# Layer 1's second query slot (QB) among the projections ahead of the scan in place of beside it, in a two-layer hybrid backbone on one core

## What is computed

```python
px = (h_x * (1.0 + ca_x) + sa_x) @ w_in[l]          # all slots of a layer at once
pc = (h_c * (1.0 + ca_c) + sa_c) @ w_in[l]
(qa, ka, va, qb, kb, vb, qc, ic, fcf, fcb, gc, qd, kd, vd) = _split_cols(px)
# group B: queries and keys with a norm per head, then the rotation
o_b = _global_attn_latent(_rope2d(nq(qb), cos, sin), _rope2d(nk(kb), cos, sin), _heads(vb), kb_c, vb_c)
# group C: a gated scan in both directions, context first, then latent tokens
f = lbd + (1.0 - lbd) * jax.nn.sigmoid(zf.astype(f32))      # zf is fcf or fcb
s_new = jnp.exp(b_last)[..., None] * s + jnp.einsum('blhk,blhv->bhkv', kc * jnp.exp(b_last[:, None] - b), vc)
```

## Time and profile before

| what | us |
|---|---|
| median of 3 runs | 2049.73 |
| lowest and highest of them | 2046.92, 2051.88 |
| the profiled execution | 2052.52 |
| its span in the profile | 2050.9 |
| TensorE busy in the span | 1927.3 |
| VectorE, GpSimd, ScalarE busy | 1294.1, 907.0, 898.8 |

### The profile page before, as it was taken

One profiled execution on the slowest core, in us unless ns is written; L12 is line 12 of the kernel. 1 busy time (PEld: TensorE's weight loads), 2 busy tenths in 40 slices (PEclk: granted clock), 3 DMA queues, 4 the chain that ended last, 5 costly groups with the idle time before them and its releaser, 6 DMA issues.

```text
span 2050.9 us, 33287 instructions
## 1 busy us (share of the span) xinstructions
PE 1927.3 (94%) x12872; PEld 1642.2 (80%) x12872; DVE 1294.1 (63%) x2519; ACT 898.8 (44%) x1917; POOL 907.0 (44%) x700
## 2 busy tenths in 40 slices
PE   6898999999999999999999998898989989999997
PEld 4787888877788888888888878798867868778886
DVE  3237888775586999999444362988786752222545
ACT  3224577567634222222243343565557534333442
POOL 2134566210154334553353334666340445675743
PEclk8999899999999999999999999999999999999999
DMA  8553010030111233323211121111130112222321
GB/s 340 204 210 122 22 43 22 22 119 2 43 62 42 106 121 124 124 87 129 93 67 68 52 103 62 42 43 42 43 119 2 63 62 99 87 87 98 124 99 66
DMA packets 26940, 177.33 MB, mean 86 GB/s; under 512 B 2720, under 2 KB 3744, under 8 KB 7712
## 3 DMA queue, kind: packets, MB, share of 16 engines
q1 hardware_dynamic: 22544, 157.90, 21.3%
q10 hardware_dynamic: 4240, 17.30, 2.1%
HBM read 171.00 MB, written 4.19 MB: 85 GB/s over the span
## 4 chain that ended last, share of the span: by engine, by line
PE 68%; DVE 15%; issue 5%; POOL 5%; ACT 4%; DMA 2%; DVEq 0%; SPq 0%; ACTq 0%; POOLq 0%
PE PS L1257 19%; PE PS L1156 18%; PE PS L872 7%; PE PS L866 5%; PE PS L1092 3%; PE PS L1117 3%; POOL WS L2341 3%; DVE W L1678 2%; DMA WR<-in_weights 2%; PE PS L1076 2%; DVE W L1995 2%; DVE W L1942 2%; PE PS L801 1%; PE PS L1005 1%; PE PS L1212 1%
## 5 line engine op out<-in xcount | busy, mean ns | idle before, releaser
L1257 PE MATMUL PS<-XH,WS 128*128 128x512 f32 x2016 | 544.5, 357 | 4.7 <-POOL WS L2341 4.7
L1257 PEld LDWEIGHTS PS<-XH,WS 128*128 128x128 f32 x2016 | 360.7, 190 | 60.4 <-issue 4.6
L1257 PE MATMUL PS<-XL,WS 128*128 128x512 f32 x1008 | 358.7, 356 | 0.0
L2341 POOL TENSOR_TENSOR WS<-WR,WS 128x1024 fp32r<-128x1024 f32 x88 | 214.8, 2442 | 295.9 <-ACT WS L1536 295.5
L1601 ACT ACTIVATE W<-PS,PR 128x768 f32<-128x768 f32 (+1 forms) x88 | 78.0, 886 | 431.3 <-PE PS L1257 362.8
L2200 DVE SCALAR_TENSOR_TENSOR W<-PS,PR,W 128x511 f32<-128x511 f32 (+1 forms) x132 | 83.0, 657 | 219.2 <-ACT W L1601 219.2
L1257 PEld LDWEIGHTS PS<-XL,WS 128*128 128x128 f32 x1008 | 191.8, 190 | 26.8
L872 PE MATMUL PS<-EU,XH 128*128 128x256 f32 x624 | 186.6, 299 | 8.0 <-issue 7.3
L2301 POOL TENSOR_TENSOR WL<-WR,EU 128x512 fp32r<-128x512 f32 x96 | 127.7, 1356 | 141.3 <-ACT EU L1316 141.1
L872 PE MATMUL PS<-WL,XH 128*128 128x256 f32 x624 | 180.6, 289 | 0.0
L872 PE MATMUL PS<-EU,HL 128*128 128x256 f32 x624 | 180.4, 289 | 0.0
(11 more groups left out here) (219 smaller groups left out, 4256.9 us busy)
## 6 DMA issues: line engine op xcount, KB each, us to landing
WR<-in_weights SPq DMA_DIRECT2D x128, 1024.0 KB, 4.8
U<-in_weights SPq DMA_DIRECT2D x16, 1024.0 KB, 6.9
U<-in_bias ACTq DMA_DIRECT2D x2, 1792.0 KB, 9.7
H<-in_x SPq DMA_DIRECT2D x1, 2048.0 KB, 10.1
H<-in_x ACTq DMA_DIRECT2D x1, 2048.0 KB, 15.1
U<-in_ln_rows ACTq DMA_DIRECT2D x2, 1024.0 KB, 4.7
WR<-in_weights SPq DMA_DIRECT2D x4, 512.0 KB, 3.6
kept<-H ACTq DMA_DIRECT2D x4, 512.0 KB, 2.6
```

Source lines behind the costliest of these rows:

```text
L1257: mm = pe.matmul(PS[u.pos][:, lo:hi], w[:, part, k, :], src[:, k, lo:hi], start=(k == 0 and src is xh3 and part == 0), stop=(k == KT - 1 a ...
L2341: pool.tensor_tensor(ws5[:, u.c % 2, 1], half_slot(u), ws5[:, u.c % 2, 0], ALU.subtract).then_inc(w_low, 1)
```

## The change

One row of the table `ORDERS` changes: in layer 1, QB moves from behind KVA to ahead of FCF.

```diff
 ORDERS = ((QC, GC, IC, QB, KVB, FCF, FCB, QA, KVA, VD, QD, KD),
-          (QC, GC, IC, FCF, FCB, QA, KVA, QB, KVB, VD, QD, KD))
+          (QC, GC, IC, QB, FCF, FCB, QA, KVA, KVB, VD, QD, KD))
```

## The result

| what | before | after |
|---|---|---|
| median of 3 runs, us | 2049.73 | 2067.50 |
| lowest and highest, us | 2046.92, 2051.88 | 2065.31, 2070.59 |
| span of the profiled execution, us | 2050.9 | 2063.7 |
| ratio after to before (95% interval) | | 1.0075 (1.0057 to 1.0093) |

The change makes the kernel slower by 0.75%, 15.4 us by the ratio and 17.8 by the medians. The prediction said slower, by 6 us, and its range ended at 2064: the sign was right and the size was not.

The account below looks back on a forecast made before the run. TensorE, busy 94% of the span, was taken as the bound. Ahead of the scan 62.0 us plus scan 164.3 made 226.3 against 220.7, about 6 us more: 2055.7 us from the median 2049.7, range 2046.5 to 2064.

Parts of the forecast that it names:

- (1): Ahead of the scan, after QB's first part: TensorE waits 0.7 us for FCF's low halves on GpSimd; between 0 and 0.8.
- (2): Ahead of the scan, past FCF's second context part: TensorE waits 0.5 us for QB's first part's rotation; between 0 and 1.
- (3): Behind FCF's first latent part: TensorE waits 6.5 us for QB's second rotation, slowed beside GpSimd's FCB low halves; 2.4 to 7.
- (4): Before FCB's first latent part: TensorE waits 4.4 us for ScalarE's take of FCB's context parts; between 3.5 and 4.8.
- the clock: Behind waits (3) and (4), ahead of the scan: lower clock costs 2 us each; between 0 and 2.6 each.
- Together 164.3: The whole scan, layer 1, to the first attention score: 164.3 us; bounds 158.5 and 171.
- iterations 0 to 3 ... 18.6: Scan's start: 11 pieces of 1.45 us and four small steps on TensorE, 18.6 us.
- 4 to 11 ... 60.0: Scan iterations 4 to 11: 5.4, 8.0, six at 7.43, and 2 for transposes, 60.0 us, against 71.8 before.
- 12 to 15: ... no wait ... 19.5: Second direction's context units: 10 pieces and small steps, no wait, 19.5 us, against 33.0 before.
- 16 to the end ... 66.2: Scan from iteration 16 to its end: 5.8, six at 8.1, 11.8, sum 66.2 us, against 72.1 before.
- D: Rival, scan: loop at 8.27 us in all sixteen output units, iteration 16 waits for ScalarE; +12 to +15; chance 0.11.
- B: Rival: no meeting in QB's second rotation, clock at 2.4 GHz, units at 7.2 to 7.6; -8 us; chance 0.12.

Follow-up runs that it names:

- e3: Changed kernel with FCB's weights split two parts later, behind own part 11 in place of 9; ratio 1.0060.
- e4: Changed kernel with ScalarE taking FCB's two context parts ahead of unit 0's exponentials in layer 1; ratio 1.0082.
- e9: e2's kernel with ScalarE's takes of FCB's context parts ahead of unit 0's exponentials; ratio 1.0000.
- e7: Changed kernel with layer 1's KVA weights split at iterations 0 and 1 and QD's at 13, each one earlier; ratio 1.0061.
- e5: Changed kernel with layer 1's KVA weights split at iterations 0 and 1 in place of 1 and 2; ratio 1.0070.
- e14: Kernel before the change, with ScalarE's copy of turned keys ahead of the exponentials for units 12 to 15 (also 2 and 3); ratio 0.9997.
- e15: e8's kernel with ScalarE's copy of turned keys ahead of the exponentials for units 12 to 15 (also 2 and 3); ratio 1.0056.
- e6: Changed kernel with layer 1's QD weights split at iteration 13 in place of 14; ratio 1.0063.
- e11: e8's kernel with the reciprocals of FCB's latent gates on VectorE replaced by a minimum (result invalid); ratio 0.9994.
- e12: Changed kernel with 24 unread products put into TensorE's 6.57 us wait before the transposes of QB part 2; ratio 1.0084.
- e8: Changed kernel with the edits of e3, e4 and e7 together (four edits); ratio 1.0033.
- e10: e8's kernel with VectorE's norm and rotation of layer 1's KVA and KVB replaced by a copy (result invalid); ratio 1.0015.
- e13: e8's kernel with TensorE leaving out one of three products per step for layer 1's KVA and KVB; ratio 1.0028.
- e2: Kernel before the change, QB still beside the scan, with only the changed kernel's staging of layer 1's forget gates; ratio 1.0007.

## Why the prediction was off, point by point

**The stretch was the right one.** 16.8 us of the difference lie in it; in front of it and behind the scores the programs differ by less than their executions do (the profiled one of after reaches the first mark 2.6 us earlier, and takes 556.7 against 558.1 from the scores on).

**The moved work and the four waits ahead of the scan** came out as written: (1) 0.67 for 0.7, (2) none for 0.5, (3) 6.57 for 6.5, (4) 4.44 for 4.4, the clock 2.9 and 1.7 for 4, and 62.9 us from IC's end (1271.71 less the 2.57 that after is ahead, to 1332.04) for 62.0. Two sizes inside (3) are off and cancel, so that its agreement is in part luck: the rotation was slowed by 3.2 us, not 4.2, and FCF's gate before it by 1.0 (1.45 for a row that alone takes 0.41). That the mechanism of (3) is the meeting, e3 shows; that (4) is the place of the take, e4 shows, and that it is worth nothing on its own, e4 and e9.

**The scan is the step that failed:** "Together 164.3", measured 174.5 (1332.04 to 1506.5), 10.2 of the 11 us by which the sum of 226.3 was short. By its four terms:
- "iterations 0 to 3 ... 18.6": 23.9. The 3.48 us wait for KVA's low halves, 0.58 for a copy, and 1.7 for 3.4 us at the lower clock. I priced it as TensorE's work and did not walk the splits of weights, which the change also moves, through ScalarE's and GpSimd's queues.
- "4 to 11 ... 60.0": 59.4.
- "12 to 15: ... no wait ... 19.5": 23.0. A wait of 3.12 and its clock.
- "16 to the end ... 66.2": 68.2 to the end of the projections, 68.7 to the scores.

**But the error was deeper than two overlooked waits.** With both edited, e7's units 0 to 3 take 18.1, below my 18.6, and its second direction 65.9, and still the scan is 171.3, the upper bound that I had given: units 4 to 15 take 87.8 for my 79.5. The first and the last term were within reach and the sum was not: I had costed them as if a wait taken out of the scan were taken out of the total. Most edits of order contradict that: 6.3 us of gain ahead of the scan gave nothing (e4), 5.8 in units 0 to 3 nothing (e5), nor did 4.7 in e9 or the copies in e14 and e15. Two did keep their gain, e3's 3.6 ahead of the scan and e6's 2.9 in the second direction. What it is in the scan that takes the others back, the two engines' loads together, the chain through a unit, or the clock that falls behind the new waits, stays open; e5 shows the clock with 3.1 of 4.8 us. The kernel before idles 17.8 us in its scan and the kernel after 15.3, though 27 us of TensorE's busy time and 34 of VectorE's have left it.

**The clock:** I had 4 us ahead of the scan, which came out, and none in it. The mean went from 0.96 to 0.93 over the whole stretch, and the same products took 7.6 us more. In the scan there are more and shorter waits, and several are followed by the lower level.

**The rivals.** D came nearest in size (+12 to +15), but not by its mechanism: the units of 4 to 11 take 7.4 us (59.4 for eight) and those of 16 to 22 7.7, not 8.27, and the stall stands at iteration 15, for unit 14's copy, not at 16. B needed no meeting and units at 7.2 to 7.6; even with the meeting gone (e3) it is far off, since the shortest scan with the changed order took 171 us (e7, e11), not 158.5.

**What stays open.** e12 and after run the same instructions from unit 16 on and differ by 4.3 us; so a difference of that size in one stretch of one profile is no proof. The 4.8 us that e5 loses behind units 0 to 3 stand better, since e7 repeats them (87.8 for units 4 to 15). e6's 2.9 us are repeated too: the six kernels with QD split earlier and nothing else moved there (e6, e7, e8, e10, e11, e13) take 65.6 to 66.2 us from unit 16 on, the five with QD's split as it was (after, e3, e4, e5, e12) 68.7 to 73.0. Not run is a kernel that lightens TensorE and VectorE at once. Why e2, with QB in the scan, gives TensorE no more idle time than the kernel before although it adds the 4.4 us wait, I can say only by the windows (units 0 to 3 without a wait), not by an experiment.

## What to carry to other kernels

Here, with engines chained through a loop at some 90% load each, TensorE work taken out of the loop came back as just that work, and the waits and the lower clock ahead of the loop were the whole price. So do not add up removed waits as if they left the total. Take work away from one engine at a time, and then from two at once: here 8 us less on either of two engines gave 1 to 2 us, while 6 us less at the loop's entrance gave 6; the run with both lighter is missing. And a table that orders projections also orders the preparation of their weights on other engines: walk those queues too.

## What the runs showed of the hardware

- A VectorE product with two inputs beside GpSimd's subtraction of low halves took 1.45 us in place of 0.38 (2.90 against 0.75 for a pair, after against e3), a row with one tensor input and scalars 1.45 in place of 0.41; reciprocals did not get longer (1.75 both ways). GpSimd's four low halves took 5.38 there, against 5.09 in the earlier trace rows. In e3 the last pair of the rotation (line 1851), at the start of the subtractions, took 1.84 in place of 0.76.
- The lower clock level set in at 1295.9, while TensorE was idle, and lasted to 1306.1, into the work from 1300.25; kept busy there in e12, TensorE stayed at the upper level through the same 10.2 us.
- Of the five waits over 1.2 us in the scan of the kernel after (3.48, 3.12, 1.33, 1.80, 1.26), four were followed by the lower level, as was one of 1.05. From unit 16 on the kernel after shows two such spells and e12, with the same instructions there, four; the stretch takes 68.7 and 73.0 us.
